# Modulation rows of a two-block model: eight summed on GpSimd, six and the value bias on VectorE

## What is computed

```python
ada = jax.nn.silu(c) @ w_ada[l] + b_ada[l]                    # 1024 x 6144, once in block 1, per layer in block 2
sh_m, sc_m, g_m, sh_f, sc_f, g_f = jnp.split(ada[:, None, :], 6, axis=-1)
h = rms_norm(x, norm_mix[l]) * (1.0 + sc_m) + sh_m
...
p = h @ w_in + b_in                                           # q, k, v, gates, hyena parts, merge gates
```

## Time and profile before

| | us |
|---|---|
| median of 3 runs (2270.08, 2271.21, 2882.92) | 2271.21 |
| the profiled execution, its own time | 2270.48 |
| its span, first to last instruction | 2268.1 |
| TensorE busy | 1904.7 (84%) |
| VectorE busy | 708.1 (31%) |
| ScalarE busy | 334.6 (15%) |
| GpSimd busy | 0.2 |
| DMA queue of the ring | 643.78 MB, 71.7% of 16 engines |

### The profile page before, as it was taken

The page is one execution under the profiler, slowest core; times in us unless marked ns, Lnnn a source line. Parts: engine busy times, 40 slices in busy tenths (PEclk is TensorE's granted clock), DMA queues, the critical chain, the costliest instruction groups (busy, mean ns, idle before and its releaser), DMA issues.

```text
span 2268.1 us, 30075 instructions
## 1 busy us (share of the span) xinstructions
PE 1904.7 (84%) x12730; PEld 1276.1 (56%) x12730; DVE 708.1 (31%) x1663; ACT 334.6 (15%) x759; POOL 0.2 (0%) x4
## 2 busy tenths in 40 slices
PE   7999999966666666666666679999999999999999
PEld 4788788511111111111111138868889978688899
DVE  3524233300000000000000035572656546625654
ACT  4132030200000000000000010260210112612100
POOL 0000000000000000000000000000000000000000
PEclk7999999988787878878787889999999999999999
DMA  9356578999999999999999995524644555246441
GB/s 322 112 216 214 179 262 321 399 428 429 428 429 428 429 429 429 428 429 429 428 429 429 428 404 175 173 76 167 241 161 164 190 194 175 86 168 231 159 167 56
DMA packets 147882, 648.59 MB, mean 286 GB/s; under 512 B 10645, under 2 KB 17410, under 8 KB 123016
## 3 DMA queue, kind: packets, MB, share of 16 engines
q1 hardware_dynamic: 144124, 643.78, 71.7%
q10 hardware_dynamic: 3660, 3.39, 0.5%
HBM read 646.10 MB, written 1.05 MB: 285 GB/s over the span
## 4 chain that ended last, share of the span: by engine, by line
PE 59%; DMA 33%; DVE 5%; ACT 2%; issue 1%; SPq 0%; ACTq 0%; DVEq 0%
DMA ring<-in_w_exp 33%; PE bank L2028 15%; PE bank L893 13%; PE bank L2711 6%; PE bank L1811 4%; PE bank L1563 4%; PE bank L2626 2%; PE bank L1826 2%; PE bank L907 1%; PE bank L936 1%; PE bank L615 1%; DVE scr L2537 1%; PE bank L771 1%; PE bank L1488 1%; PE bank L934 1%
## 5 line engine op out<-in xcount | busy, mean ns | idle before, releaser
L1811 PE MATMUL bank<-ring,arena 128*32 128x512 f32 x1968 | 307.7, 760 | 203.9 <-DMA ring<-in_w_exp 193.5
L1811 PEld LDWEIGHTS bank<-ring,arena 128*32 128x32 f32 x1968 | 61.3, 124 | 431.7 <-DMA ring<-in_w_exp 310.3
L893 PE MATMUL bank<-hx,ring 128*128 128x256 f32 x1344 | 293.2, 379 | 0.7 <-ACT hx L789 0.7
L893 PEld LDWEIGHTS bank<-hx,ring 128*128 128x128 f32 x1344 | 254.6, 190 | 37.5 <-issue 3.4
L1826 PE MATMUL bank<-ring,arena 128*32 128x512 f32 x1008 | 158.4, 768 | 82.7 <-DMA ring<-in_w_exp 71.8
L1869 DVE COPY arena<-bank 128x256 f32<-128x256 f32 x16 | 6.8, 424 | 525.3 <-PE bank L1816 525.3
L2028 PE MATMUL bank<-arena 128*128 128x256 f32 x672 | 151.0, 379 | 0.3 <-DVE arena L2077 0.3
L1826 PEld LDWEIGHTS bank<-ring,arena 128*32 128x32 f32 x1008 | 32.1, 130 | 191.4 <-DMA ring<-in_w_exp 112.7
L2028 PEld LDWEIGHTS bank<-arena 128*128 128x128 f32 x672 | 127.0, 190 | 17.5 <-DVE arena L2077 0.6
L1876 DVE COPY arena<-bank 128x256 f32<-128x256 f32 x16 | 6.8, 424 | 345.7 <-PE bank L1700 345.7
L2028 PE MATMUL bank<-ring,hx 128*128 128x256 f32 x448 | 105.8, 379 | 0.0
(11 more groups left out here) (486 smaller groups left out, 2284.4 us busy)
## 6 DMA issues: line engine op xcount, KB each, us to landing
ring<-in_w_exp SPq DMA_DIRECT2D x186, 2048.0 KB, 16.2
ring<-in_w_ada SPq DMA_DIRECT2D x36, 2048.0 KB, 11.9
ring<-in_w_in SPq DMA_DIRECT2D x29, 2048.0 KB, 9.0
ring<-in_w_ffn_in SPq DMA_DIRECT2D x20, 2048.0 KB, 7.9
ring<-in_w_ffn_out SPq DMA_DIRECT2D x10, 2048.0 KB, 7.7
ring<-in_w_out SPq DMA_DIRECT2D x6, 2048.0 KB, 10.9
arena<-in_w_exp SPq DMA_DIRECT2D x4, 2048.0 KB, 19.3
ring<-in_w_up_nsa SPq DMA_DIRECT2D x2, 2048.0 KB, 8.3
```

Of the source, the lines that this page charges most:

```text
L893: ins = pe.matmul(b[:, o:o + n], w[:, k, j * P:(j + 1) * P], h[:, k, :], start=k == 0, stop=k == KD - 1)
L1811: ins = pe.matmul(banks[s][32 * j:32 * j + 32, :], e_xe[:, 2 * t + kk, :], w[:, kk, 512 * j:512 * j + 512], start=t + kk == 0, stop=t + kk ...
```

## The change

- **VectorE** multiplies and adds later0 to later5: eight operations a tile, each of 512 elements a partition, into an accumulator (`dve_later_sum`). later0 and 1 fill the four `after` places of v's sums, later2 and 3 stand between the row chain and the copy of tokc, later4 and 5 between context and conv 4.
- **GpSimd** does later8, 10, 12 and 14 and the two late pairs of the attention passes, in place in the ring slot (`pool_row`): eight multiplies of 512, then adds of 2048, 1024 and 512.
- **TensorE** then adds up over the partitions with a matrix of ones: 4 matmuls a tile in place of 32. later6, 7, 9, 11, 13 and 15 and the other late pairs stay as they were.
- A tile summed on VectorE is free when VectorE has read it, one on GpSimd when TensorE has.
- `pe_later` for later2 and 3 moves from between hy0 and hy1 to behind the context.
- The value bias is loaded to all partitions and added by VectorE; its six matmuls go. The state products wait for the new last sum, and so does ScalarE's first copy of the later rows.

```diff
@@ -182,7 +182,7 @@
     adarow = view(arena, 16548, P, 2, P)
     pre = view(arena, 16804, P, 2, 4, N)
     post = view(arena, 18852, P, 2, 4, N)
-    bvrow = arena[0:1, 23992:24504]
+    bvrow = arena[:, 23992:24504]
...
     def act_ml_loads(act):
-        act_load(act, "load_ml", bvrow, A["b_in"][0:1, ML0 + 1024:ML0 + 1536])
+        act_load(act, "load_ml", bvrow, A["b_in"][0:1, ML0 + 1024:ML0 + 1536].broadcast_to([P, 512]))
...
                 claim(pe, 6, f"later rows{g}")
+            if i < ON_DVE:
+                pe.wait_ge(*at(f"later summed{i}"))
+                for j in range(4):
+                    ins = pe.matmul(banks[6][32 * j:32 * j + 32, (i % 4) * P:(i % 4 + 1) * P], ones[:, 0:32],
+                                    later_acc[i][:, j // 2, (j % 2) * P:(j % 2 + 1) * P], start=True, stop=True)
+                ins.then_inc(*PE.step(f"full later rows{g}"))
+                continue
             w = tile(pe, f"later{i}")
+            if i in ON_POOL:
+                pe.wait_ge(*at(f"later summed{i}"))
+                for j in range(4):
+                    ins = pe.matmul(banks[6][32 * j:32 * j + 32, (i % 4) * P:(i % 4 + 1) * P], ones[:, 0:32],
+                                    w[:, 0, j * P:(j + 1) * P], start=True, stop=True)
+                ins.then_inc(*PE.step(f"full later rows{g}"))
+                mark_used(pe, f"later{i}")
+                continue
...
+    ON_DVE = 6
+    ON_POOL = (8, 10, 12, 14)
+
+    def pool_row(g, key, m, name):
+
+        w = tile(g, key)
+        for k in range(KD):
+            g.tensor_scalar(w[:, k, :], w[:, k, :], cT[:, k, m:m + 1], None, ALU.mult).then_inc(*PO.step())
+        for half in (4, 2, 1):
+            g.wait_ge(*PO.last())
+            g.tensor_tensor(w[:, 0:half, :], w[:, 0:half, :], w[:, half:2 * half, :], ALU.add).then_inc(*PO.step(name))
...
+    def pool_later(g):
+        PO.stage("ada")
+        g.wait_ge(*at("c columns"))
+        for i in ON_POOL:
+            pool_row(g, f"later{i}", 0 if i < 8 else 2, f"later summed{i}")
+
+    def pool_late(g, n):
+        PO.stage("late")
+        for i in range(2):
+            pool_row(g, f"late{n}_{i}", 2, f"late summed{n}_{i}")
+
+    later_acc = [arena[:, 14368 + 512 * i:14880 + 512 * i].rearrange("p (a b) -> p a b", a=2) for i in range(2)]
+    later_acc += [hcx[:, 2 * i:2 * i + 2, 0:N] for i in range(4)]
+
+    def dve_later_sum(v, i, part):
+
+        w = tile(v, f"later{i}")
+        acc = later_acc[i]
+        if part == 0 and i > 1:
+            v.wait_ge(*at("full gates"))
+        for k in (0, 1, 2, 3) if part == 0 else (4, 5, 6, 7):
+            c = cT[:, k, 0:1]
+            x = w[:, k, :].rearrange("p (a b) -> p a b", a=2)
+            if k == 0:
+                v.tensor_scalar(acc, x, c, None, ALU.mult).then_inc(*DV.step())
+            else:
+                v.wait_ge(*DV.last())
+                v.scalar_tensor_tensor(acc, x, c, acc, ALU.mult, ALU.add).then_inc(*DV.step())
+        if part:
+            book.where[f"later summed{i}"] = DV.now
+            book.where[f"used {where[f'later{i}']}"] = DV.now
+
...
     def act_later(act, g):
-        act.wait_ge(*at("m3 v"))
+        act.wait_ge(*at("v sums"))
...
         b = bank(pe, f"late rows{g}")
         for i in range(2):
             w = tile(pe, f"late{g}_{i}")
+            if g in (1, 4):
+                pe.wait_ge(*at(f"late summed{g}_{i}"))
+                for j in range(4):
+                    ins = pe.matmul(b[32 * j:32 * j + 32, i * P:(i + 1) * P], ones[:, 0:32], w[:, 0, j * P:(j + 1) * P],
+                                    start=True, stop=True)
+                ins.then_inc(*PE.step(f"full late rows{g}"))
+                mark_used(pe, f"late{g}_{i}")
+                continue
...
@@ -934,9 +1001,6 @@
                         ins = pe.matmul(o, x[:, k, j * P:(j + 1) * P], h[:, k, :], start=start, stop=True, skip_group_check=True)
                     else:
                         ins = pe.matmul(o, h[:, k, j * P:(j + 1) * P], x[:, k, :], start=start, stop=True, skip_group_check=True)
-                if key == "v" and bias is not None:
-                    ins = pe.matmul(o, ones[0:1, 0:P], bvrow[:, 256 * bias:256 * bias + 256], start=False, stop=True,
-                                    skip_group_check=True)
...
                 f = lambda x: x.rearrange("p (c h e) -> p c h e", c=2, h=2)
+                with_bias(u.rearrange("p (c n) -> p c n", c=2), nh)
+                v.wait_ge(*DV.last())
                 v.tensor_tensor((vc, vx)[th][:, :, 2 * nh:2 * nh + 2, 0:P], f(b), f(u), ALU.add).then_inc(*DV.step(*names))
+
+        def with_bias(x, nh):
+            v.tensor_tensor(x, x, spread(bvrow[:, 256 * nh:256 * nh + 256], 1, 2), ALU.add).then_inc(*DV.step())
 
...
+        if key == "v":
+            v.wait_ge(*at("v copied"))
+            for c in range(NC):
+                x = vc[:, c, 0:2, 0:P]
+                v.tensor_tensor(x, x, bvrow[:, 0:256].rearrange("p (h e) -> p h e", h=2), ALU.add).then_inc(
+                    *DV.step("v sums"))
...
         pe_later(pe)
         pe_linear_T(pe, "hy0_", "hy00", x, N)
-        pe_later(pe)
         pe_linear_T(pe, "hy1_", "hy10", x, N)
         pe_context(pe)
+        pe_later(pe)
         pe_linear_T(pe, "hy2_", "hy20", x, N)
...
-        dve_seven_wide(v, "v", lambda i: None)
+        dve_seven_wide(v, "v", lambda i: dve_later_sum(v, i // 2, i % 2))
         dve_conv(v, 1)
         dve_rows(v)
+        for i in (2, 3):
+            dve_later_sum(v, i, 0)
+            dve_later_sum(v, i, 1)
+        dve_tokens(v)
         dve_conv(v, 2)
         dve_conv(v, 3)
         dve_context(v)
+        for i in (4, 5):
+            dve_later_sum(v, i, 0)
+            dve_later_sum(v, i, 1)
         dve_conv(v, 4)
         dve_later(v, 0)
         dve_conv(v, 5)
...
+    @block.gpsimd
+    def _(g):
+        pool_later(g)
+        for l in range(LAYERS):
+            pool_late(g, 3 * l + 1)
```

14 lines of the change are left out of this document (7 added, 7 removed).

## The result

The changed kernel takes 2288.46 us (median of 4 runs, 2285.99 to 2290.96), the kernel before 2271.36: a ratio of 1.0077, with a 95% interval of 1.0065 to 1.0089. It is slower by 17 us where 8 us less were forecast. The interval leaves 15 to 20 us, so this is far clear of it, though the prediction took 45 us (2%) for the least that can be told from no change. Each round of experiments measured the kernel before again (medians of 2270.56 to 2271.93 us), and each ratio is to that of its own round. The profiled execution took 2290.96 us, its span is 2288.7, 20.6 more than before.

A forecast was written before the change was run, and what follows sets the result against it. The chain was read as 59% TensorE and 33% expert tiles coming from memory. Gains of 16.4 us less 3.4 for the clock and 5.0 for VectorE left 8.0: 2270.5 became 2262.5 us, range 2250 to 2276.

The forecast's parts named there:

- VectorE beside GpSimd: GpSimd's work hindering VectorE: 5 us lost, 1 in the head chain and 2 in each attention pass.
- Part 1, value bias: Stage of v: six bias matmuls leave TensorE, 4.7 us gained; VectorE's added work costs 0.
- Part 2: later0 and later1, after the gate rows, summed on VectorE: 3.1 us gained.
- Part 3: later2 and later3 moved behind the context: 3.1 us gained, but a new 2.6 us wait for hy1's tile, bounds 0 to 5.
- Part 4: later4 and later5 behind o: TensorE's 3.1 us turn into waiting before the last hyena turn, gain 0.
- Part 5: GpSimd rows in the first block: later8 gains 1.6 us, later10 and later12 0, later14 0.3.
- R = 15: GpSimd's time for one tile, taken as 15 us; up to 18 costs nothing, each us above it 2 us.
- rival B: GpSimd blocks VectorE for whole operations, costing 16.4 us, mostly at the compressed keys' chain: 2274 us; chance 0.26.
- rival C: GpSimd's row too long for the ring, TensorE waits at later14: slower from R = 22, 2318.5 us at R = 36; chance 0.05.
- Part 6: Late tiles of the two attention passes on GpSimd: 3.1 us gained in each, 6.2 in all.
- clock 3.4: Lower granted clock after new idle spells of TensorE: two of three at 1.7 us, 3.4 us lost.
- Rival A: GpSimd does not hinder VectorE, idle more than half of the time there in the passes: 2257.5 us; chance 0.27.

The follow-up runs named there:

- f3: The kernel before with only the value bias moved from TensorE's matmuls to VectorE: 2265.24 us, ratio 0.9975.
- f1: e1 with hy1's weight tile asked for ahead of later2 and later3: 2262.39 us, ratio 0.9962.
- f2: f1 with VectorE's conv 5 ahead of the rows' addition: 2255.78 us, ratio 0.9930.
- k3: k2 with rows 8, 10 and 12 of the first block also made on VectorE: 2252.07 us, ratio 0.9912.
- k2: f2 with the two rows of each attention pass made on VectorE in its idle gaps: 2249.98 us, ratio 0.9911.
- h1: The changed kernel with GpSimd's additions left out, so its rows are not summed: 2261.71 us, ratio 0.9960.
- k4: h1 with two GpSimd multiplications of 2048 elements a row in place of eight of 512: 2274.89 us, ratio 1.0019.
- e3: The changed kernel with GpSimd only in the attention passes, its first-block rows back on TensorE: 2279.36 us, ratio 1.0040.
- e1: The changed kernel without any GpSimd row, those rows back on TensorE; VectorE's sums, order and bias stay: 2267.84 us, ratio 0.9987.

## Why the prediction was wrong

The forecast was 2262.5 us, the range 2250 to 2276; 2288.5 lies outside it. The step that failed is the 5 us put down for VectorE beside GpSimd: it was 18.4. In the profiled executions the step from a gain of 8.0 to a loss of 20.6 us is 28.6 us. Step by step:

- **Part 1, value bias, 4.7 us: right, 0.9 too low.** TensorE leaves the stage of v 5.6 us earlier (118.68 against 124.25), and by itself the bias is worth 5.6 us (f3). VectorE's added work cost nothing there.
- **Part 2, 3.1 us: right** (hy0 starts 8.6 us earlier for 7.8 forecast).
- **Part 3: the new wait was mis-sized.** It was put at 2.6 us, with three tiles at 385 GB/s. SP asked for hy1's tile at 135.68, the time forecast, but it was there only at 154.86 instead of 153.4, and hy0 ended 0.8 us earlier than forecast. The wait was 4.83 us, near the upper bound of 5; another 2.7 us went to hy1's low clock, so the two took 7.5 of the 12.2 us gained up to there (hy1 could have begun at 150.0, before it began at 162.2). f1 shows that the order of the tiles is the cause: both are gone.
- **Part 4, 0: right.** The pair behind o gave a wait of 3.10 us (3.8 forecast); f2 shows it was VectorE's order.
- **Part 5, rows 10 and 12 at 0: right** (k3, which adds row 8 at 1.6, wins nothing from the three). **R = 15: wrong**; it measured 20.7, the value of the scan row, which stood there as a bound. The additions took what rival B supposed, 4.5, 2.4 and 1.4 us, but a multiplication took 1.58 us where 1.0 was supposed. The consequence was worked out beforehand, "each us above it 2 us": 2 x (20.7 - 18) = 5.4 us, and TensorE waited 5.41 us for row 14. That it fits to a hundredth is in part luck: the room is 36.2 us as forecast, but it lies 8.1 us later, from 302.60 to 338.78 in place of 294.5 to 330.7. This is rival C's place and price, below its threshold.
- **Part 6, 6.2 us: the saving was right, and the change lost it again.** TensorE's 3.1 us are there in each pass once nothing holds VectorE (k2, and nearly so h1). In the change it spends 0.65 us on the pair too, but waits longer for VectorE on the way.
- **What is given back, clock 3.4: too little.** hy1 lost 2.7, the transform 1.6 (8.77 against 7.13), head 1 and the merge product behind it 2.6, row 15 behind the wait for row 14 1.3 (3.61 against 2.30 in h1) and the branch product 1.7 us, 9.9 in all. The number of spells was a guess: after a wait of 2.12 us at head 1 the clock was down here, after one of 2.13 us at the same place it was not in h1:

```profile
303.89 0.49 PE L1471 MATMUL bank<-arena 128*128 128x129 f32 x2 [2.13 <-DVE arena L1510]
...
306.23 13.98 PE L957 MATMUL bank<-hx,ring 128*128 128x256 f32 x64
```

- **What is given back, VectorE beside GpSimd, 5: the step that failed.** In the passes the change lost 7.6 and 4.2 us and its saving of 3.1 in each, 18.0 in place of 4. In the first pass 6.8 of 10.7 us are longer waits for VectorE, and most of the rest is the clock behind them: 30 to 62 us after the first product its mean was 0.84 in both passes, before 0.95. In the head chain, 1 forecast, it is the 0.4 us at head 3 (4.15 against 3.78 in h1). Together 18.4 us, 13.4 more than forecast.

13.4 for VectorE, 5.4 for row 14, 2.2 for hy1's wait and 6.5 for the clock are 27.5 us. The stretch from the branch product's end to the first pass, with the experts in it, took 1.6 us longer, and the bias gave 0.9 more than forecast: 28.2 of the 28.6 us. Why the experts took longer stays open.

The likeliest case was taken to be "nearer to 0 since all rows at hand show VectorE unhindered". But no row showed GpSimd at work at all, so nothing spoke for that end. Rival A's support, that the passes leave VectorE idle more than half of the time, holds for 1467 to 1497 us of the trace of before (busy 13.8 of 30 us), but not behind it: busy 23.0 of the 32 us from 1485.7 on. With rows of 20.7 us GpSimd worked from 12 to 54 us after the pass's first product, not from 11 to 41, and so into that part.

Rival B had the mechanism, and its price of 16.4 us was near the 18.4; its 2274 lacks row 14, hy1 and the rest of the clock. It supposed that the additions have to meet the short chain of the compressed keys. They met its end here (L2420), but need not: VectorE scales scores between SBUF and SBUF (L2643) in the second half of the pass, TensorE waits for them, and the second row's additions met them there.

The Trainium skill (SBUF: State Buffer, Who interferes with whom) gave the rule: a VectorE instruction with two SBUF inputs, or in its two-port mode, and a GpSimd instruction that reads SBUF exclude each other for the whole instruction, and one with a single SBUF input outside such modes contends with nothing. By that rule the traces agree on the additions (4.08 us held in one of 4.5) and on VectorE's operations that read a PSUM bank (0.28 us under an addition). On short multiplications they differ: these read SBUF as well, and 99.5 us of them held VectorE for 6 us. They differ from "for the whole instruction" in k4 as well, where L2403 went through before the multiplication beside it had ended. There the measurement decides.

What stays open: why a multiplication of 512 elements lets VectorE through and one of 2048 or an addition of 512 does not, and why in k4 a held operation went through some 1.6 us before the multiplication's end. No run here tells these.

## What to carry to other kernels

An engine that stands idle is not free if its work reads the same memory as an engine for which the bottleneck waits: before giving rows to GpSimd, list the partner's operations between SBUF and SBUF in that stretch, and count them as held for as long as the additions run. Compare first with the idle gaps of the faster engine: a row that cost GpSimd 20.7 us fitted into a 6.45 us gap of VectorE. The passes' four rows lost 11.5 us on GpSimd (e3 against e1) and won 5.8 on VectorE (k2 against f2; 4.3 by the ratios). And when work is taken from the bottleneck, the next tile and the next partner must be moved up with it: two lines of order (f1, f2) were worth 12 us, four times the 3 us that the VectorE part of the change won without them (e1).

## What had not been expected of the hardware

- A GpSimd multiplication of 128x512 by a column takes 1.58 us, an addition of two tiles of that size 1.36: with one operand it is the slower one. Four times the size take 5.46 and 4.52 us.
- What a GpSimd multiplication costs VectorE depends on its length: 0.06 us for each us of 1.58 us multiplications, 0.29 for each us of 5.46 us ones. With additions it does not: 0.32 for each us of 1.30 us ones, 0.31 for long ones.
- Under a GpSimd addition a VectorE operation of 30 elements took 4.06 us, and the next one, which reads a PSUM bank, 0.29 us.
- After many of TensorE's waits the granted clock was at its lower level, 1.2 GHz, for a while, but not after all of them: from 304 to 308 us, behind equal waits at head 1, it was 0.50 of the full 2.4 GHz in the changed kernel and 1.00 in h1. A mean of 0.57 was seen in the 4 us about the wait at head 3, and the product after hy1's wait took 16.74 us for 14.08. The changed kernel in the stretch of head 3 (columns as in the earlier trace rows):

```profile
334.00:338.00 4.00, 3.06 (x15) 3.06 (x16) 3.79 (x11) 0.03 (x1) 3.92 (x3) 0.57 1.02 404
```
